# Both mixers' output products by token tile, in a two-block transformer kernel on one core

## What is computed

```python
# first block
h = layer_norm(x) * (1 + sc1) + sh1
merged = sigmoid(g_ssd) * y_ssd + sigmoid(g_att) * y_att    # state-space branch, attention branch
y = merged @ w_o                                            # 256x1024 @ 1024x1024
x = layer_norm(ALPHA * x + (1 + gt1) * y, ln1_g, ln1_b)
h = layer_norm(x) * (1 + sc2) + sh2
y = hierarchical_moe(h, ...)      # top-2 of 16 experts, 1024x512, 1024x512, 512x1024 each
x = layer_norm(ALPHA * x + (1 + gt2) * y, ln2_g, ln2_b)
# second block
h = rmsnorm(x, g_norm_mix) * (1 + sc1) + sh1
x = x + gt1 * ((g_a * o_a + g_b * o_b) @ w_out)             # 256x1024 @ 1024x1024
h2 = rmsnorm(x, g_norm_ffn) * (1 + sc2) + sh2
x = x + gt2 * expert_choice_ffn(h2, ...)   # 16 experts of 32 tokens, 1024x2048, 1024x2048, 2048x1024 each
return rmsnorm(x, g_final)
```

## Time and profile before

| | us |
|---|---|
| median of three runs | 2225.66 |
| the profiled execution, its own time | 2228.3 |
| its span, first to last instruction | 2226.5 |
| PE busy in the span | 1654.4 (74%) |
| DVE busy | 442.5 (20%) |
| ACT busy | 288.0 (13%) |
| first mixer's output product, from start to end | 416.3 to 445.7 |
| first block's expert rounds begin | 495.0 |
| second mixer's output product, from start to end | 1221.9 to 1251.5 |
| second block's expert rounds begin | 1288.2 |

### The profile page before, as it was taken

The page is one execution under the profiler, slowest core; times in us unless marked ns, Lnnn a source line. Parts: engine busy times, 40 slices in busy tenths (PEclk is TensorE's granted clock), DMA queues, the critical chain, the costliest instruction groups (busy, mean ns, idle before and its releaser), DMA issues.

```text
span 2226.5 us, 19952 instructions
## 1 busy us (share of the span) xinstructions
PE 1654.4 (74%) x8097; PEld 862.8 (39%) x8097; DVE 442.5 (20%) x890; ACT 288.0 (13%) x602; POOL 103.9 (5%) x99
## 2 busy tenths in 40 slices
PE   6899999969999699999997755645465544554444
PEld 2675654444443477687754421311121111211111
DVE  6430532252222322121325300000000000000001
ACT  6211222020000222122223100000000000000000
POOL 7000000000000100111111000000000000000000
PEclk9999999979999799999998777768778777877777
DMA  8899543719998342443452469999999999999995
GB/s 276 295 332 340 179 157 138 301 67 408 424 428 344 128 151 76 165 138 132 137 167 109 193 293 428 428 428 428 428 427 427 428 427 428 428 428 428 428 428 248
DMA packets 116171, 670.55 MB, mean 301 GB/s; under 512 B 8643, under 2 KB 11400, under 8 KB 85360
## 3 DMA queue, kind: packets, MB, share of 16 engines
q1 hardware_dynamic: 111568, 657.50, 72.9%
q0 software_dynamic: 3744, 11.11, 1.6%
q10 hardware_dynamic: 768, 0.64, 0.1%
HBM read 661.88 MB, written 7.34 MB: 301 GB/s over the span
## 4 chain that ended last, share of the span: by engine, by line
PE 60%; DMA 30%; DVE 4%; ACT 2%; issue 1%; SPq 1%; POOL 0%; DVEq 0%; ACTq 0%; POOLq 0%
PE psum L906 13%; PE psum L896 12%; DMA ring<-in_w_up 10%; DMA ring<-in_w_down 10%; PE psum L1392 10%; DMA ring<-in_w_gate 9%; PE psum L1204 5%; PE psum L1234 2%; PE psum L864 2%; PE psum L1174 2%; PE psum L1244 1%; PE psum L1127 1%; SPq L635 1%; PE psum L1327 1%; DVE h_tok L177 1%
## 5 line engine op out<-in xcount | busy, mean ns | idle before, releaser
L1392 PE MATMUL psum<-work,prob 128*32 128x512 f32 x1024 | 290.8, 733 | 158.5 <-DMA ring<-in_w_up 84.6
L1392 PE MATMUL psum<-ring,prob 128*32 128x512 f32 x1024 | 290.9, 733 | 146.9 <-DMA work<-in_w_up 85.0
L906 PE MATMUL psum<-ring,hT 128*128 128x512 f32 x672 | 304.9, 600 | 3.2 <-ACT hT L177 2.2
L896 PE MATMUL psum<-hT,ring 128*128 128x256 f32 x1152 | 277.7, 386 | 1.5 <-DVE hT L177 1.5
L896 PEld LDWEIGHTS psum<-hT,ring 128*128 128x128 f32 x1152 | 214.1, 193 | 36.2 <-issue 10.5
L1392 PE MATMUL psum<-work,hT 128*32 128x512 f32 x512 | 139.0, 705 | 87.7 <-DMA ring<-in_w_down 87.7
L1392 PE MATMUL psum<-ring,hT 128*32 128x512 f32 x512 | 139.0, 704 | 56.3 <-DMA work<-in_w_down 53.0
L906 PEld LDWEIGHTS psum<-ring,hT 128*128 128x128 f32 x672 | 124.6, 192 | 135.8 <-issue 133.7
L1392 PEld LDWEIGHTS psum<-work,prob 128*32 128x32 f32 x1024 | 71.3, 132 | 264.3 <-issue 264.3
L1392 PEld LDWEIGHTS psum<-ring,prob 128*32 128x32 f32 x1024 | 71.4, 132 | 249.2 <-issue 249.2
L177 ACT ACTIVATE work<-psum 128x512 f32<-128x512 f32 (+2 forms) x99 | 56.2, 567 | 609.1 <-PE psum L1378 236.6
(11 more groups left out here) (322 smaller groups left out, 1618.4 us busy)
## 6 DMA issues: line engine op xcount, KB each, us to landing
ring<-in_w_gate SPq DMA_DIRECT2D x40, 2048.0 KB, 19.0
work<-in_w_up SPq DMA_DIRECT2D x40, 2048.0 KB, 20.3
work<-in_w_gate SPq DMA_DIRECT2D x40, 2048.0 KB, 19.9
ring<-in_w_up SPq DMA_DIRECT2D x40, 2048.0 KB, 20.7
ring<-in_w_down SPq DMA_DIRECT2D x40, 2048.0 KB, 20.0
work<-in_w_down SPq DMA_DIRECT2D x40, 2048.0 KB, 19.8
ring<-in_w_in SPq DMA_DIRECT2D x72, 1024.0 KB, 7.4
ring<-in_w_mod SPq DMA_DIRECT2D x24, 1024.0 KB, 8.7
```

What stands on the lines that cost most here:

```text
L896: mm = pe.matmul(o[:, wide(j * S, S)], w[:, ch], actT[:, c, :], start=(c == 0), stop=(c == KC - 1))
L906: mm = pe.matmul(o, actT[:, c, wide(t * P, P)], w, start=(c == 0), stop=(c == KC - 1))
L1392: mm = pe.matmul(o[wide(i * CAP2, CAP2), :], lhs(chunks_per * piece + c, i), R.slot(l + i, (chunks_per, width))[:, c, wide(b * BANK, BANK) ...
```

## The change

Each mixer's product is taken tile by tile: transposes of tile 0, the wait for its two copies, half 0 and half 1 of tile 0, then the same for tile 1. DVE empties the jobs in that order, and in the second block it runs `rms_modulated` for a tile right after that tile's second job. In the second block the transposes of tile 0 for the router (`h4T_0`) stand ahead of the spread of row 11, those of tile 1 behind it, and ACT empties row 11 between them. The last reader of a weight chunk is now the job of tile 1.

```diff
+        def plan_by_tile(transposed, name, w):
+            for t in range(TT):
+                jobs(f"{transposed}_{t}", 2)
+                for i in range(D // BANK):
+                    jobs(f"{name}_{i}_{t}", 1)
+            for i in range(D // BANK):
+                load_chunk(f"{name}_{i}", w, wide(i * BANK, BANK), job(name, 2 * i + TT - 1))
...
-        jobs("mT", 4)
-        plan_chunks("w_o", A["w_o"][0], 0, 2)
+        plan_by_tile("mT", "w_o", A["w_o"][0])
...
-        jobs("mixT", 4)
-        plan_chunks("w_out", A["w_out_2"][0], 0, 2)
+        plan_by_tile("mixT", "w_out", A["w_out_2"][0])
+        jobs("h4T_0", 2)
         plan_spread(11)
-        jobs("h4T", 4)
+        jobs("h4T_1", 2)
...
+            def by_tile(transposed, name, src, ready):
+                for t in range(TT):
+                    transpose_tokens(transposed, src, ready, (t,))
+                    for half in range(2):
+                        pe.wait_ge(*emptied(job(transposed, 2 * t + half)))
+                    for i in range(D // BANK):
+                        in_one(token_job(name, i, t, hT))
...
-            transpose_tokens("mT", h, "merged_ready")
-            for k in range(4):
-                pe.wait_ge(*emptied(job("mT", k)))
-            token_major("w_o", 2, hT)
+            by_tile("mT", "w_o", h, "merged_ready")
...
-            transpose_tokens("mixT", h, "mix_ready")
-            for k in range(4):
-                pe.wait_ge(*emptied(job("mixT", k)))
-            token_major("w_out", 2, hT)
+            by_tile("mixT", "w_out", h, "mix_ready")
+            transpose_tokens("h4T", h, "h4_ready", (0,))
             spread(11)
-            transpose_tokens("h4T", h, "h4_ready")
+            transpose_tokens("h4T", h, "h4_ready", (1,))
...
-            for n in range(2):
-                take(job("mod11", n), mod[:, 2, wide(n * BANK, BANK)])
             for j in range(4):
                 t, half = divmod(j, 2)
+                if j == 2:
+                    for n in range(2):
+                        take(job("mod11", n), mod[:, 2, wide(n * BANK, BANK)])
...
-                n, t = divmod(j, 2)
-                cols, k = wide(n * BANK, BANK), job("w_o", j)
+                t, n = divmod(j, 2)
+                cols, k = wide(n * BANK, BANK), job("w_o", 2 * n + t)
...
-                n, t = divmod(j, 2)
-                cols, k = wide(n * BANK, BANK), job("w_out", j)
+                t, n = divmod(j, 2)
+                cols, k = wide(n * BANK, BANK), job("w_out", 2 * n + t)
...
-            rms_modulated(4, "h4_ready")
+                if n:
+                    rms_modulated(4, "h4_ready", (t,))
```

More of the change, by code:

```diff
@@ L877, in spread, with transpose_tokens @@
                         end(pe.matmul(o, select[:, n * 16 + u:n * 16 + u + 1].to_broadcast([P, P]), mod_rows[:], start=True, stop=True))
-            def transpose_tokens(name, src, ready):
-                for t in range(TT):
+            def transpose_tokens(name, src, ready, tiles=range(TT)):
+                for t in tiles:
                     pe.wait_ge(signal(ready), t + 1)
@@ L2100, in _, with rms_modulated @@
                 normalize(x, 6 + t, t, params[:, 0, :], params[:, 1, :], (signal("x_b1_ready"), t + 1), y_sum)
-            def rms_modulated(n, ready):
-                for t in range(TT):
+            def rms_modulated(n, ready, tiles=range(TT)):
+                for t in tiles:
                     step(v.tensor_tensor, h[:, t, :], x[:, t, :], mod[:, 1, :], ALU.mult)
```

## The result

The changed kernel takes 2213.65 us (median of five, 2212.55 to 2215.75) against 2225.66 us before; the ratio is 0.9949, 95% interval 0.9938 to 0.9959. That is 12.0 us less, where 11.4 was forecast. A second measurement of the same two kernels on another occasion gave 2214.3 against 2225.3, ratio 0.9947 (0.9934 to 0.9961), where the same 0.9949 was expected.

What follows compares the result with a forecast made beforehand. The chain from mixer product to first expert product, which releases the weight stream, was taken as the bound. First mixer 5.0, second mixer's product 4.1 and norm 2.3 sum to 11.4 us: 2225.66 - 11.4 = 2214.3 us, range 2210.5 to 2220.2.

Steps and rivals of the forecast that it cites:

- What bounds it: Both blocks: the weight stream's start hangs on the chain to the first expert product; every microsecond taken there shortens the end.
- the idle stretch: DMA engines stand still before each layer's ninth load, so issuing loads 6 and 7 later was costed at nothing.
- First mixer, 5.0 us: First block's mixer: tile 0's norm hides under tile 1's products, whose chain starts at 444.3 instead of 449.3; gain 5.0 us.
- Second mixer, the product, 4.1 us: Second block's mixer: products start 6.4 us earlier, with a break between tiles, and end at 1247.4, not 1251.5; gain 4.1 us.
- Second mixer, the norm, 2.3 us: Second block: tile 0's modulation hides under tile 1's products; the router product starts 7.5 us after their end, not 9.8.
- The clock at the breaks: Rival, both mixers: the clock drops behind each break, costing 1.9 us each; gain only 5.7, 2220.0 us; chance 0.17.
- The slower rival: Ring slots, both blocks: later release of loads 6 and 7 delays the whole stream by 7.6 us; 2233.3 us; chance 0.02.
- Only the second mixer's part arrives: Rival, first expert stage: transfers set its end from an unmoved start, so the 5.0 us are lost; 2219.3 us; chance 0.09.
- the working of the loads: SP's weight loads: load 6 goes out 5.0 and 2.6 us later, second chunk wanted 6.9 us earlier; costed at nothing.

Runs made afterwards that it cites:

- the order alone: The changed kernel, but all transposes and waits come first as in the kernel before, then the products in the new order; 2217.1 us, ratio 0.9961.
- the second mixer alone: The changed kernel with the first mixer put back as in the kernel before, only the second by token tile; 2218.76 us, ratio 0.9965.
- the first mixer alone: The changed kernel with the second mixer put back as in the kernel before, only the first by token tile; 2220.96 us, ratio 0.998.
- the one with 3.54: The changed kernel with tile 1's transposes issued three times in both mixers, making the break 3.54 us instead of 2.02; 2216.17 us, ratio 0.9962.
- the fastest one: The changed kernel with tile 1's transposes between tile 0's two products in both mixers, and ACT emptying row 11 last; 2209.24 us, ratio 0.9932.

## Why the prediction was right

- **What bounds it.** Right. The last stage's length did not change by 0.2 us, and each mixer alone arrived at the end with its own part. Holding back loads 6 and 7 by up to 26 us cost nothing, so the idle stretch was the cover that it was said to be. The first expert products came at 487.65 and 1275.51 and not at 490.0 and 1276.8. In the first block the 7.4 us from 495.02 are the mixer's 5.2 and 2.2 in the stretches before and behind it; up to the second block's, 1.2 of these 2.2 are gone again.
- **First mixer, 5.0 us.** It was 5.2. The step that mattered was DVE being 3.6 us late; the run with the order alone isolates it. The working had the start 1.8 us earlier and a break of 2.3, a loss of 0.5; measured are 4.07 - 2.03 = 2.0 and 2.0, and the two cancel. Both terms were off for one reason: I took the wait behind ACT's last copy as it was before, 416.31 - 415.95 = 0.36, and it is 413.11 - (411.72 + 1.28) = 0.11 now. The remaining 1.7 us is the fall of the clock that the profile before shows. I had 1.92, from the timeline's 29.40 and the chain's 27.48; in the timeline the product at 892 reads 27.63 and that of the order alone 27.70. I counted it as a sure gain, but with the same 4.07 us stretch it came in the kernel before and with the second mixer alone (29.40 us each) and not with the order alone (27.70). That part of the 5.0 depends on the execution. In the medians the first mixer alone gave 4.6.
- **Second mixer, the product, 4.1 us.** It was 4.4. The break was sized 2.3 and took 2.0, and the start came 2.7 us after the first transpose instead of 2.9, by the same shorter wait.
- **Second mixer, the norm, 2.3 us.** It was 2.1. ACT's copies of tile 1 ended at T + 7.5 instead of T + 7.1 and came last, behind row 11's copies; tile 1's second transposes were ready at T + 5.9 and not T + 6.6, since the clock was not at half there. That the placement of row 11's spread costs nothing was right for the change as it stands; the same order costs 2.1 us where tile 0's norm is late.
- **The clock at the breaks.** It did not fall. None of the profiles with the two-microsecond break shows tile 1's products longer than 13.97 us, nor does the one with 3.54. The rule of the Trainium skill (TensorE: Matmul & The Clock Gate, section "HAM oscillation — how this bites in real kernels") names a true cost, seen at 417 in the earlier trace rows; no break here paid it. That is no proof that a longer one is safe: with the same 4.07 us of transposes and waits two profiles show the fall (the granted clock is 0.50 at 417 and, with the second mixer alone, at 419) and one does not. What decides between them is not shown.
- **The slower rival**, a stream delayed by the later slots, was refuted by its own run. "Only the second mixer's part arrives" fell with the first mixer alone.

One line in the working of the loads is wrong and cost nothing: the second weight chunk is wanted about 10 us earlier than before and not 6.9, since its first reader was the third job, from about 432 on, and is now the second. It was issued at 388.40.

The median came out 0.65 us under the forecast. That closeness is in part luck: the three terms were off by +0.2, +0.3 and -0.2 us, and unchanged stretches vary by more than that. In the two profiles 11.7 of the 12.6 us are the change's and the rest is in stretches that it doesn't touch.

## What to carry to other kernels

Look where the next long stage's stream stands still: here time taken from the chain that releases it arrived at the end in full, however small the share of busy time was. When a product is followed by a per-tile norm, order it by tile if the vector engine is late at its end, and put the next tile's transposes between two products of this tile, so that the copies are covered (1.2 us a mixer in the stretches here). Before moving a side job in an in-order queue, ask what it would stand behind if the tile ahead of it were late.

## What was not expected of the hardware

- TensorE idled 1.24 us between the transposes and the product where it waited for four emptied banks (the kernel before, and the order alone), and 0.97 to 0.98 us where it waited for two. The second mixer has the same step: 1.00 us with four waits and 0.73 with two. Counted from the end of ACT's last copy, it is 0.36 us with four waits and 0.10 or 0.11 with two, in both mixers. The number of waits is the difference in the code; that it is the cause was not tested by itself.
- Unchanged stretches come in two lengths. From the first expert product of the first block to the first `mixT` transpose the profiles show 717.2 to 717.5 us in some kernels (the kernel before and the fastest one among them) and 718.7 to 719.0 in the others. The last stage, from the second layer's first product to the end, takes 936.9 to 939.4 us over the fourteen profiles, in kernels with the same code there. One profile thus can't part kernels 1.5 us apart by its span, while the stretches of the changed code agree within 0.3 us from run to run.
